# Modulation chunks in groups, and q/k started on half of its weights, in a two-layer GLA, short-conv and expert kernel on one core

## The reference, cut to what matters

```python
for i in range(DEPTH):                        # 2 layers, 256 context + 256 latent tokens, width 1024
    sh1, sc1, gt1, sh2, sc2, gt2 = split(silu_c @ w_mod[i] + b_mod[i], 6)      # for x
    csh1, ..., cgt2 = split(silu_cc @ w_mod[i] + b_mod[i], 6)                  # for the context
    p  = modulate(rmsnorm(x, g_mix_pre[i]), sh1, sc1) @ w_in[i]    # q k v g a_f a_b B C h
    pc = modulate(rmsnorm(xc, g_mix_pre[i]), csh1, csc1) @ w_in[i]
    # chunked gated linear attention in both directions from q, k, v and the decays,
    # short convolution B * conv(C * h), both times their gates -> mixed
    x = x + gt1 * rmsnorm(mixed @ w_out[i], g_mix_post[i])          # the context too, in layer 0
    h = modulate(rmsnorm(x, g_ffn_pre[i]), sh2, sc2)
    x = x + gt2 * rmsnorm(ffn(h), g_ffn_post[i])   # layer 0: SwiGLU; layer 1: top 2 of 8 experts
```

## Time and profile before

| what | value |
|---|---|
| median of 3 runs | 1739.92 us (1739.76 to 1742.04) |
| the profiled execution's own span | 1737.8 us |
| TensorE busy | 1638.6 us, 94% of the span |
| VectorE, ScalarE busy | 955.3 us, 536.7 us |
| DMA | 476.26 MB, mean 274 GB/s |
| first q/k product, end of q/k | 39.84 us, 63.5 us |
| first expert product | 874 us |

### The profile page before, as it was taken

One profiled execution on the slowest core, in us unless ns is written; L12 is line 12 of the kernel. 1 busy time (PEld: TensorE's weight loads), 2 busy tenths in 40 slices (PEclk: granted clock), 3 DMA queues, 4 the chain that ended last, 5 costly groups with the idle time before them and its releaser, 6 DMA issues.

```text
span 1737.8 us, 21264 instructions
## 1 busy us (share of the span) xinstructions
PE 1638.6 (94%) x8432; PEld 1123.6 (65%) x8432; DVE 955.3 (55%) x1343; ACT 536.7 (31%) x682; POOL 4.0 (0%) x13
## 2 busy tenths in 40 slices
PE   6999999999999999998999999999989999888886
PEld 3788666788888885797788834887338873333322
DVE  4588775544445776699598712986129951110102
ACT  4421243400000005414577502774027730000001
POOL 0000000000000000000000000000000000000000
PEclk9999999999999999999999999999999999999999
DMA  9320785333321316327599999999999999999996
GB/s 360 136 97 1 283 299 189 102 97 97 97 97 37 133 58 236 102 94 291 216 411 372 353 384 408 412 408 411 415 407 412 409 410 411 407 412 409 411 414 265
DMA packets 160619, 476.26 MB, mean 274 GB/s; under 512 B 10002, under 2 KB 33012, under 8 KB 146164
## 3 DMA queue, kind: packets, MB, share of 16 engines
q1 hardware_dynamic: 158688, 474.24, 71.1%
q10 hardware_dynamic: 1812, 0.41, 0.1%
HBM read 473.58 MB, written 1.05 MB: 273 GB/s over the span
## 4 chain that ended last, share of the span: by engine, by line
PE 72%; SPq 14%; DVE 5%; DMA 5%; issue 3%; ACT 2%; ACTq 0%; DVEq 0%; POOL 0%; POOLq 0%
SPq L785 11%; PE ps L918 10%; PE ps L920 10%; PE ps L919 10%; PE ps L1376 7%; PE ps L1368 6%; PE ps L1370 6%; PE ps L1276 6%; SPq L789 3%; PE ps L1316 2%; PE ps L882 2%; PE ps L841 2%; DMA ring<-in_e_w 1%; DMA work<-in_e_w 1%; DMA ring<-in_w_in 1%
## 5 line engine op out<-in xcount | busy, mean ns | idle before, releaser
L1276 PE MATMUL ps<-ring,work 128*64 128x512 f32 x960 | 223.5, 614 | 32.8 <-DMA ring<-in_e_w 30.3
L2534 DVE TENSOR_TENSOR norms<-work,ps 64x256 f32<-64x256 f32 x70 | 29.7, 424 | 324.5 <-ACT work L1839 323.0
L918 PE MATMUL ps<-ring_rounded 128*128 128x512 f32 (+1 forms) x536 | 190.6, 356 | 2.9 <-DVE norms L2316 1.6
L1276 PEld LDWEIGHTS ps<-ring,work 128*64 128x64 f32 x960 | 73.7, 141 | 169.7 <-issue 166.7
L1978 DVE TENSOR_TENSOR ring_rounded<-ring,hT_rounded 128x2048 fp32r<-128x2048 f32 x72 | 163.0, 2287 | 16.9 <-ACT hT_rounded L1862 16.8
L920 PE MATMUL ps<-ring_rounded 128*128 128x512 f32 (+1 forms) x472 | 163.3, 346 | 0.0
L1862 ACT CAST hT_rounded<-ring 128x2048 fp32r<-128x2048 f32 x72 | 136.6, 1914 | 33.3 <-PE ps L1370 18.7
L920 PE MATMUL ps<-mixT_rounded,ring_rounded 128*128 128x512 f32 x328 | 127.6, 389 | 0.0
L918 PE MATMUL ps<-mixT_rounded,work_rounded 128*128 128x512 f32 x304 | 118.3, 389 | 0.0
L919 PE MATMUL ps<-hT_rounded,work_rounded 128*128 128x512 f32 x304 | 118.3, 389 | 0.0
L918 PEld LDWEIGHTS ps<-ring_rounded 128*128 128x128 f32 x536 | 101.3, 189 | 19.5 <-issue 2.4
(11 more groups left out here) (307 smaller groups left out, 2866.5 us busy)
## 6 DMA issues: line engine op xcount, KB each, us to landing
ring<-in_e_w SPq DMA_DIRECT2D x288, 1024.0 KB, 18.4
ring<-in_w_mod SPq DMA_DIRECT2D x24, 2048.0 KB, 11.0
ring<-in_w_in SPq DMA_DIRECT2D x12, 2048.0 KB, 8.9
mixT<-in_e_w SPq DMA_DIRECT2D x24, 1024.0 KB, 18.5
work<-in_e_w SPq DMA_DIRECT2D x24, 1024.0 KB, 18.6
ring<-in_w SPq DMA_DIRECT2D x22, 1024.0 KB, 7.8
ring<-in_w_out SPq DMA_DIRECT2D x4, 2048.0 KB, 15.2
ring<-in_w SPq DMA_DIRECT2D x4, 2048.0 KB, 7.7
```

The costliest lines, as they stand in the source:

```text
L918: pe.matmul(acc, w_high_, x_high_, start=first, stop=False)
L1276: ins = pe.matmul(narrow_bank(b)[H * w:H * w + H, :], xsel[:, k, 0:H], piece_words(e, pair[w])[:, at_:at_ + BLK], start=(k == 0), stop=(k ...
```

## The change

Four things are done. (1) The start's chunks become two groups: (0,0) and (0,2) first, then the upper four rows of the q/k weights (1 MB, a semaphore of its own), then (0,1), (0,3) and the rest of q/k. The q/k products of k = 0 to 3 run with the first group; the *late* group is multiplied at k = 2 and k = 4, and ScalarE's modulation takes it at k = 4. (2) The squares of the first norm are added by VectorE, and TensorE makes two products instead of eight; ScalarE empties the banks of the odd `xT` tiles. (3) All chunks of a place are multiplied into one bank: the two vectors stand in `csil` with zero columns around them, and the weights' window is moved by two columns for each chunk, so that each chunk fills rows of its own. One copy and one group of transposes then serve the whole place: 11 instead of 24. entry and entry1 are joined to residual and second. (4) The transposes of keys, added, residual, second, keys1 and last are put behind other work, and some banks are chosen anew.

```diff
+MODS = {"start": ((0, 0), (0, 2)), "late": ((0, 1), (0, 3)), "keys": ((0, 4), (0, 5)), "added": ((0, 6), (0, 7)),
+        "states": ((0, 8), (0, 9)), "outputs": ((0, 10), (0, 11), (1, 0)), "residual": ((1, 1), (1, 2), (1, 3)),
+        "second": ((1, 4), (1, 5), (1, 6)), "keys1": ((1, 7), (1, 8)),
         "states1": ((1, 9),), "last": ((1, 10), (1, 11))}
...
         for i in range(4):
-            use(("U", L, 0, i), rot())
+            use(("U", L, 0, i), rot() if L else (turn[0] + 1 + i % 3) % 4)
+        if L == 0:
+            mod_col("added", turn[0] % 4)
         for i in range(4):
             use(("U", L, 1, i), 4 + i)
         if L == 0:
-            mods("states")
+            mods("states", (4, 5))
...
+    chunk_order.remove(("qk", 0))
+    chunk_order.insert(2, ("qk", 0))
...
+                if ch == ("qk", 0):
+                    sp.dma_start(d3[:, 0:PAIRS], rows(w_in[0][0:D // 2], COL["qk"], 512)).then_inc(first_half_in, 16)
...
+                if ch == ("mod", *MODS["late"][1]):
+                    sp.dma_start(rest_of, rows(w_in[0][D // 2:], COL["qk"], 512)).then_inc(
+                        chunk_in[slot_of["qk", 0]], 16)
...
+            def mod_row(ch):
+                group = GROUP_OF[ch]
+                n = group.index(ch)
+                acc = begin(("mrow", *group[0])) if n == 0 else bank(("mrow", *group[0]))
+                w = weights(("mod", *ch))
+                for kk in range(2):
+                    for g in range(4):
+                        k = 4 * kk + g
+                        o = csil_at + 32 * k - 2 * n
+                        ins = pe.matmul(acc[32 * g:32 * g + 32, :], csil[:, o:o + 32], w[:, k, :],
+                                        start=(n == 0 and kk == 0), stop=(ch == group[-1] and kk == 1),
+                                        skip_group_check=True)
+                end(ins)
...
+            mod_row(MODS["start"][0])
+            last_square(("ssq", 0), TOK)
+            mod_row(MODS["start"][1])
+            mod_col(MODS["start"])
...
                 for k in range(KD):
+                    if late and k == 2:
+                        mod_row(late[0])
+                    if late and k == 4:
+                        mod_row(late[1])
+                        mod_col(late)
...
-                mods("residual" if L == 0 else "last")
-                square_sum(("ssq", 2 * L + 1), KD, n)
+                place = MODS["last" if L else "residual"]
+                for ch in place[0:2]:
+                    mod_row(ch)
+                for k in range(KD):
+                    if k == 2 and place[2:]:
+                        mod_row(place[2])
+                    if k == (3 if L else 6):
+                        mod_col(place)
+                    add_square(("ssq", 2 * L + 1), k, KD, n)
...
+            for k in range(KD):
+                if k % 2 == 0:
+                    wait_tile(act, ("xt", k + 1))
+                    drains(act.copy(xT[:, k + 1, :], bank(("xt", k + 1))[:]), ("xt", k + 1))
+                wait_drained(act, ("xt", k))
+                square(xT[:, k, :], TOK)
+            inverse_rms(("ssq", 0), TOK, D)
+            take_rows(MODS["start"])
...
+                    elif norm == 0 and k == 4:
+                        take_rows(MODS["late"])
+                        act.wait_ge(mod_ready, len(MODS["start"] + MODS["late"]))
...
+            for k in range(0, KD, 2):
+                wait_tile(dve, ("xt", k))
+                drains(dve.tensor_copy(xT[:, k, :], bank(("xt", k))[:]), ("xt", k))
+                if k:
+                    add_one_square(("ssq", 0), k // 2 - 1, TOK)
+            for k in range(KD // 2 - 1, KD - 1):
+                add_one_square(("ssq", 0), k, TOK)
...
             for p in range(PAIRS):
                 split_in(("qk", 0, p))
+                if p == 2:
+                    take_mods(MODS["late"])
...
-                take_mods(*MODS["keys1" if L else "keys"])
                 conv(3)
-                if L == 0:
-                    take_mods(*MODS["added"])
+                take_mods(MODS["keys1" if L else "keys"])
...
                     dve.tensor_copy(small[:, 14, 3 + d:4 + d], ones[:, 0:1]).then_inc(states_ready, 1)
+                    if L == 0 and d == 0:
+                        take_mods(MODS["added"])
```

More of the change, by code:

```diff
@@ L54 @@
 VROWS = 113
-MODS = {"start": ((0, 0), (0, 1), (0, 2), (0, 3)), "keys": ((0, 4), (0, 5)), "added": ((0, 6), (0, 7)),
-        "states": ((0, 8), (0, 9)), "outputs": ((0, 10), (0, 11), (1, 0)), "residual": ((1, 1), (1, 2)),
-        "entry": ((1, 3),), "second": ((1, 4), (1, 5)), "entry1": ((1, 6),), "keys1": ((1, 7), (1, 8)),
+MODS = {"start": ((0, 0), (0, 2)), "late": ((0, 1), (0, 3)), "keys": ((0, 4), (0, 5)), "added": ((0, 6), (0, 7)),
+        "states": ((0, 8), (0, 9)), "outputs": ((0, 10), (0, 11), (1, 0)), "residual": ((1, 1), (1, 2), (1, 3)),
+        "second": ((1, 4), (1, 5), (1, 6)), "keys1": ((1, 7), (1, 8)),
         "states1": ((1, 9),), "last": ((1, 10), (1, 11))}
+GROUPS = list(MODS.values())
+GROUP_OF = {ch: group for group in GROUPS for ch in group}
+ROW_SLOTS = 4
 SLOTS = 4
@@ L222, in rot, with mod_row, mod_col, mods @@
         return (turn[0] - 1) % 4
[L224 to L237, removed]
+    def mod_row(ch, bank):
+        use(("mrow", *ch), bank if ch == GROUP_OF[ch][0] else None, ("mod", *ch))
+    def mod_col(place, bank):
+        use(("mcol", *MODS[place][0]), bank)
+    def mods(place, banks):
+        for ch in MODS[place]:
+            mod_row(ch, banks[0])
+        mod_col(place, banks[1])
     use(("vec", 0), 6)
@@ L242, in plan @@
     start = MODS["start"]
[L243 to L249, removed]
+    mod_row(start[0], 5)
+    use(("ssq", 0), 4)
+    mod_row(start[1], 5)
+    mod_col("start", 6)
+    for ch in MODS["late"]:
+        mod_row(ch, 5)
+    mod_col("late", 7)
     for L in range(DEPTH):
@@ L252, in plan @@
         if L:
+            mod_row(MODS["second"][2], 5)
+            mod_col("second", 6)
             use(("ssq", 2 * L), 4)
-            mods("entry1", (6, 7))
         for m in range(RT):
@@ L299, in plan @@
         use(("yss", 2 * L), 4)
-        if L == 0:
-            mods("residual", (6, 7, 0, 1, 2, 3))
-        else:
-            mods("last", (6, 7))
+        place = "last" if L else "residual"
+        for ch in MODS[place]:
+            mod_row(ch, 6)
+        mod_col(place, 7)
         use(("ssq", 2 * L + 1), 5)
         if L == 0:
-            mods("entry", (6, 7))
             for j in range(JF):
@@ L313, in plan @@
             use(("yss", 1), 4)
-            mods("second", (5, 6, 7))
+            for ch in MODS["second"][0:2]:
+                mod_row(ch, 5)
     for i in range(2):
@@ L332, in hybrid_backbone @@
     for n, (name, bank, chunks) in enumerate(uses):
-        tile_at[name], bank_of[name], nth_of[name] = n, bank, count[bank]
-        count[bank] += 1
+        tile_at[name], bank_of[name] = n, bank
+        if bank is not None:
+            nth_of[name] = count[bank]
+            count[bank] += 1
         for ch in chunks:
@@ L1047, in _ @@
                     scores(s + 1, lvl[:, s % 2, 1], lvl[:, s % 2, 0])
-                mods("keys1" if L else "keys")
+                place = MODS["keys1" if L else "keys"]
+                for ch in place:
+                    mod_row(ch)
                 pe.wait_ge(state_ops, 4 * L + 2)
@@ L1058, in _ @@
                     end(ins)
+                mod_col(place)
                 if L == 0:
-                    mods("added")
+                    for ch in MODS["added"]:
+                        mod_row(ch)
                 for d in range(2):
+                    if L == 0 and d == 1:
+                        mod_col(MODS["added"])
                     for i in range(4):
@@ L1174, in _ @@
                     added_squares(("yss", 1), 4, TOK)
-                    mods("second")
+                    for ch in MODS["second"][0:2]:
+                        mod_row(ch)
             pe.wait_ge(gate_diag_ready, 1)
```

160 lines of the change are left out of this document (72 added, 88 removed).

## The result

| | kernel before | changed kernel |
|---|---|---|
| median of 12 runs | 1741.46 us (1739.76 to 1742.73) | 1743.97 us (1740.59 to 1747.05) |
| ratio, 95% interval | | 1.0016 (1.0009 to 1.0024) |
| span of the profiled run | 1737.8 us | 1743.0 us (its time: 1744.81) |

The change costs 2.5 us where a gain of 2.0 was forecast. That is 0.14%, inside the 0.2% that the prediction calls no change, but the interval leaves 1 out, and the time lies above the range of 1734.0 to 1742.5. It is 6.1 above the forecast of 1737.9. Some 1.5 us of that is the base: 1739.92 was the median of three runs; twelve runs give 1741.46, and those beside the experiments 1740.81 to 1741.84. The other 4.5 are the change's own.

A forecast was written before the change was run, and what follows sets the result against it. TensorE, 72% of the chain, was taken as the bound, with gains possible only before the router. Terms of -3.7 us and one slow stretch of +1.7 gave -2.0: span 1735.8, median 1737.9 us, range 1734.0 to 1742.5.

The forecast's parts named there:

- The start: First norm and q/k: q/k starts at 29.45 and ends at 60.6 before any slow stretch, a gain of 2.9 us.
- The price of a fall: TensorE's granted clock dropping to half behind a pause: each slow stretch costs 1.7 us.
- states: Layer 0's state rows wait for bank 4: +0.5 us; without that wait the stage would gain 2.7.
- residual: Norm 1 with entry joined: three chunks' rows ahead of or within the squares, +0.6 us, between +0.3 and +2.
- second: Norm 2 with entry1 joined: +0.4 ahead of the squares' end, entry1's copy gone, +0.1 us in all.
- keys1: Layer 1's keys: conv(3) goes ahead of the second transpose, so the state chain begins 0.5 earlier: -0.5 us.
- last: Squares ahead of the router: three follow the chunk rows at once, one group of transposes, -1.5 us.
- I count one fall on the path: Whole path: one drop to half clock behind the new pauses, +1.7 us; chance 0.37 as the forecast.
- the edit makes three new pauses: TensorE idle about 2.2 us at 19.0, about 2.9 at 45.9, and 2.6 in the states stage.
- rival (a): No drop to half clock behind the new pauses: -3.7 us, 1736.2; chance 0.20.
- Rival (b): Two or three drops to half clock: -0.3 to +1.4 us, 1739.6 to 1741.3; chance 0.23.
- Rival (c): Removed transposes pay in full, bank of states free in time, no clock drop: -7.5 us, 1732.4; chance 0.12.

The follow-up runs named there:

- e3: Changed kernel with the third chunk of residual and of second put back behind the squares; 1740.63 us, ratio 0.9991.
- e4: Kernel before with only the start's part of the change, every later place as it was; 1741.73 us, ratio 1.0000.
- e5: Changed kernel with both late chunks multiplied ahead of q/k row 2 and their transposes ahead of row 3; 1737.64 us, ratio 0.9976.
- e8: Changed kernel with the edits of e2, e3 and e5 together and no added products; 1732.28 us, ratio 0.9937.
- e10: Changed kernel with seven products that nobody reads behind the squares of norm 2 alone; 1741.41 us, ratio 1.0003.
- e1: Changed kernel with products that nobody reads filling four TensorE pauses (late transposes, rows of states, norms 1 and 2); 1737.56 us, ratio 0.9978.
- e2: Changed kernel with the rows of states in a bank of the rotation in place of bank 4; 1740.96 us, ratio 0.9992.
- e12: Changed kernel with unread products at the start alone: five ahead of the first norm's sum, six behind the transposes; 1741.87 us, ratio 1.0000.
- e9_router_filled: e6_all_filled with four more unread products between the last routing product and the first gather; 1732.94 us, ratio 0.9954.
- e6_all_filled: Changed kernel with e5's order, e2's bank and unread products at the first norm's sum, the start's transposes and both later norms; 1730.25 us, ratio 0.9930.
- e7: Kernel before with eight unread products ahead of its first q/k product; 1741.84 us, ratio 0.9999.
- e11: e7 with three and one more unread products at two waits ahead of the squares of norm 2; 1740.33 us, ratio 0.9999.

## Why the prediction was wrong

By its own steps:

- **The start** was right: q/k from 29.54 (29.45 put), row 4 at 49.82 (49.4), the fall at 52, end 62.58 (60.6 + 1.7 = 62.3). What was missing is that its first pause, "about 2.2 us at 19.0" (2.6 measured), can be followed by a fall of its own: q/k then starts at 30.5 to 31.2 in place of 29.4 to 30.1 (e3, e4, e5, e8, e10).
- **The price of a fall**, 1.7 us, was right for three of the changed kernel's four: 1.6, 1.5 and 1.9 by e1. It is no constant (0.4 and 0.5 ahead of layer 1 in e2 and e12). Behind residual it was 0.5, since there the products run into the wait for unit 3's split, which was 0.94 before.
- **states** was right: +0.5 put, +0.7 in e1, where the wait stands and the clock doesn't fall; the rows came at 214.16 (215.05 put, less the 0.88 that q/k had gained). "If the bank wait weren't there, the stage would gain 2.7" was too much: by its own terms (+0.5 less the 2.6 from 212.5 to 215.1) it is 2.1, and to y e2 gains 1.3.
- **residual** was right: +0.6 put, +0.5 to unit 3 in e1 (+1.1 with the fall). The load of its third chunk was issued at 287.00 and landed 7.8 us later, at 294.8; its rows began at 295.07, at once behind the second square, so it cost nothing. The landing was well taken: 294 is 8.5 behind y, 8.0 was measured. The estimate of 6.8 us by the Trainium skill (DMA: Bandwidth & Descriptors, Anatomy of one DMA) is a microsecond short here; that fit is of DMAs that GpSimd issues, and SyncE issues this one. **second**: +0.1 put, 0.0 measured to its end. **outputs** and the **expert loads**: 0 put; the last product has 0.6 more offset than the first of expert 0. Over all profiles that difference is -0.8 to +1.3, while the offset at expert 0 goes from -10.3 to +5.6: time won or lost before the router is kept to the end, as was said.
- **keys1** (-0.5 put) gave -0.3, **last** (-1.5 put) gave -0.9; so it is in all the kernels here that keep them, except that in e5 and e8 a slow stretch at 796 to 804 took keys1's back. Right in sign, together 0.8 too large.
- **"I count one fall on the path"** is the step that failed, and with it what leads up to it: "the edit makes three new pauses", and "all lie between the row that fell and the one that didn't". The second is misread: of 2.2, 2.9 and 2.6 us only the 2.2 lies between 1.44 and 2.43; the other two are longer than the 2.43 that fell, so these rows alone spoke for two falls. And the edit makes five pauses of 1.77 us and more, not three. I looked for pauses where the edit adds a wait, and took the work that it removes behind the squares as an instruction count (the terms of residual and second). But these rows and transposes were the filling of a wait that was there all the time. The cost of taking them out stood in no term. The profiled run then had four falls behind new pauses (two of the three forecast ones, and both that were not), 1.6 + 1.5 + 0.5 + 1.9 = 5.5 us in place of 1.7, and a longer slow stretch in the router, +1.75.

Without falls the sum is -0.88 - 1.63 = -2.5 for the start, +0.7, +0.6, 0, -0.3, -0.9: -2.4, against -3.7 put. With 5.5 and 1.75 it is +4.8; the table has +4.75 at the first expert product. That the last two agree is no test, since the falls are what e1 doesn't have. A test is the median of e1, the change without its four falls: 4.3 below the kernel before on its chip, near the 3.7 of rival (a) (its profile has only -2.3 at expert 0, beside a trace that is 1.8 below its median). Rival (b), two or three falls, was the right mechanism with too small a number. The medians differ by only 2.5, since the trace of the kernel before is of a fast run of it and the changed kernel's of a slightly slow one. How many falls a median run has is not known, as only one run of each was profiled.

The router's part is not shown to be the change's: from the gate products to the first expert product profiles of kernels with the same router need 17.8 (e1) to 20.4 us (e4), by where the clock falls in it and comes back; the one of the kernel before needs 18.2. Rival (c), the removed transposes paying in full, failed on its condition: the bank wait came as written out, and where the bank was free (e2) the stage gained 1.3, not 2.7. That e8 is 9 us below the kernel before doesn't bear it out, since e8 also moves the late group and the third chunks.

## What to carry to other kernels

Before instructions that stand between two dependent stages are moved or joined, read what idle time they cut up: a wait of 0.80 + 0.36 us with work in it was not followed by a fall in any profile here, the same wait in one piece of 3.44 us was in eight of nine, and put up to 6 us of the next products at half clock. Work that isn't needed at once is worth leaving in such a wait; it costs nothing there (e3_rs_apart), and where there is none, products that nobody reads do the same (e1_fill), though not where the clock has fallen already (e9_router_filled). Take the base of a forecast from more than three runs when the change is worth less than their spread.

## What the chip showed that I had not expected

- A pause of 1.77 us (rows of *states*) was followed by 1.2 GHz in the profiles of the changed kernel, e3 and e10, and not in those of e5 and e12 (rows in 3.64). One of 3.44 us (layer 1) was in the changed kernel, e2 and e12, and not in e5. In the earlier trace rows 2.43 fell and 1.44 did not, but a pause of 1.03 us was followed by a fall in e8 (206 us) and one of 1.17 us ahead of layer 1's U products in e5 and e8 (0.50 from 800 and 798), and not in the changed kernel. A wait cut by transposes was followed by one too: 0.71 + 2.20 us at the late group in all six profiles that have it unfilled, 1.36 + 0.82 us at 676 us in e4 and e7, though not in the kernel before. So the length of the pause alone doesn't decide it.
- The granted clock also fell with no pause ahead of it: in the router's products of 8 columns while TensorE was busy for all of the window (e9, 850 to 852, 0.62), where e6_all_filled kept 1.00 through the same products.
- The stall of 1.8 us inside a chunk's products, in the same place in e7 and e11, which differ by a few products, and in no other kernel; not explained.
